# First modulation vectors of a two-block network: half as rows on VectorE, half as columns on TensorE, with the opening transfers on one queue

## The chip, the cores and the metric

The kernel runs on one core of one Trainium2 chip. The metric is the device time of one execution in microseconds (us), lower is better. The engines are PE (TensorE, matmuls), DVE (VectorE), ACT (ScalarE), POOL (GpSimd) and SP (SyncE, here only for issuing transfers). Each has its own instruction stream; they wait for one another on semaphores.

## What is computed

Two blocks of two layers each work on a sequence of 256 tokens of width 1024, all in float32; the first layer also carries a context sequence of 256 tokens. The prologue, which the change concerns, is the start of layer 0:

```python
m_lat = split(silu(c)     @ ada_w[0] + ada_b[0], 9)   # nine vectors of 1024: shift, scale, gate, ...
m_ctx = split(silu(c_ctx) @ ada_w[0] + ada_b[0], 9)
def half_ffn(h, m, off, g, w_gu, w_down):
    y = rmsnorm(h, g) * (1 + m[off + 1]) + m[off]
    return h + 0.5 * m[off + 2] * swiglu(y, w_gu, w_down)
h_ctx = half_ffn(ctx, m_ctx, 0, ...)                  # 256 tokens of the context
h_lat = half_ffn(x,   m_lat, 0, ...)                  # 256 tokens
```

Further on the context uses m_ctx[3] and m_ctx[4] for the mixer of layer 0. m_ctx[5] to m_ctx[8] reach no output, since nothing reads the context's residual after that mixer. Behind this stand the rest of four layers (mixers with scans, a convolution, gated linear attention, attention, and seven more feed-forward halves).

## The kernel before

Channels lie on the 128 partitions, so a vector of 1024 is 8 columns, called tiles here; the nine modulation vectors are MT = 72 tiles, in MOD[:, m, tile], with m = 0 for layer 0 and m = 4 for the context. X holds both sequences (the second is the context), Y the normalised input of the next product, PREW the first weights of the modulation (in ARENA), W two slots for weights, ADAW two slots for modulation rows, CB the vectors c and c_ctx copied to all partitions, CT the table of constants, VEC all small vectors.

The modulation is computed in two ways. The first 16 tiles (shift and scale of the first norm) are products on PE: `columns(c)` (L2377 to L2381), called for c = 0 to 3, has 4 blocks of 128 outputs by 8 blocks of the sum, each a 128x128 weight with a moving operand of only 2 columns (c and c_ctx); `first_mods` (L2722) adds the bias from PSUM. All other tiles are dot products by rows on DVE: `ada(g)` (L2689) takes a group of 4 tiles from an ADAW slot, multiplies each 128x1024 tile by the broadcast vector and accumulates, once for c_ctx into JUNK (L2705, layer 0 only) and once for c (L2708). POOL issues the loads of these groups, two ahead (L2333), and begins when PE has finished all four `columns`. The groups are spread over the feed-forward halves by lists of numbers, one for each unit; the first feed-forward takes 50 of the 68.

A feed-forward of both sequences has 11 units of gate and up products (L2402, four PSUM tiles of 128x512 each) and 4 units of down products (L2422).

The order before the first feed-forward is this. SP issues X, then four pieces of column weights, then the first weights. ACT issues VEC, CT and the two rows of CB, computes silu of c and c_ctx (L2650, L2651), squares X into Y (L2608), later takes the root (L2617) and silu of CB (L2675). PE waits for CT, runs `columns(0)` and `columns(1)`, then the sum of squares as 8 products with a matrix of ones (`total`, L2523), then `columns(2)` and `columns(3)`. DVE in `first_rms` inverts the root (L2919), normalises Y (L2922), waits in `first_mods`, forms the scales (L2937) and applies scale and shift to 16 blocks of 256 tokens (L2930). PE begins the first unit as soon as the first quarter of these is there.

Of the kernel before, what the change touches and what calls it, by code (L numbers as in the profile page):

```python
# [23 lines left out]
PRE_COLS = 512  # L24
PRE_TILES = PRE * PRE_COLS // P
GROUP = 4
SLOT = FT * 2 * P
# [21 lines left out]

ADA_GROUPS = [(0, tile) for tile in range(PRE_TILES, MT, GROUP)]  # L50
ADA_GROUPS += [(layer, tile) for layer in range(1, 4) for tile in range(0, MT, GROUP)]
LAYER_GROUPS = [sum(of <= layer for of, _ in ADA_GROUPS) for layer in range(4)]


def constant_table():
# [12 lines left out]
    add("ones", np.ones((P, P)))  # L68
    half = np.kron(np.eye(2), np.ones((HD, HD)))
# [42 lines left out]
    add("eps", np.tile(np.array([[1e-6, 64e-5, 1e-5 / ALPHA ** 2, 1e-5, 1.0, 0.0, np.pi / 2]]), (P, 1)))  # L112
# [41 lines left out]
def build(nc, t, out, table_at, stop=None):  # L154

    stop = STOP if stop is None else stop
    with ExitStack() as ctx:
# [6 lines left out]
        ncols = table_at["resident"][1]  # L164
# [44 lines left out]
        s_tab = sem("table_loaded")  # L209
# [519 lines left out]
        def rwkv_pe(pe, mm, ph):  # L729
            m = mixers["rwkv"]  # L730
            for seq in range(2):
# [6 lines left out]
                def tile(f):  # L738
# [8 lines left out]
                    if seq == 1 and n_ == 0:  # L747
                        pe.wait_ge(s_yl, 1)
# [1385 lines left out]
        group0 = 0  # L2134
# [46 lines left out]
        def norm(layer, k, T, of=None):  # L2181
            n_rs = sum_squares(T, 1.0 / D, "rms")
            if of:
                add("first_sums", of)
            n["nx"] += PIECES if n["y"] else 0
            add("rms", layer, 3 * k, T, n_rs, vec("norm_g", 24 * layer + 8 * k, 8), bump("y"), n["nx"])
# [142 lines left out]
        def _(pool):  # L2329
# [19 lines left out]
            for g in range(F[1]["group0"]):  # L2349
# [16 lines left out]
        def _(pe):  # L2366
# [18 lines left out]
            def ffn(sec, n_y):  # L2385
                T, w0, t0, per = sec["T"], sec["w0"], sec["t0"], sec["per"]

                def unit(u, dyn):
# [3 lines left out]
                    for q in range(2):  # L2392
                        for g in range(2):
# [132 lines left out]
            pe.wait_ge(s_tab, 16)  # L2526
            pe.wait_ge(s_sc, 1)
            columns(0)
            columns(1)
            first = True  # L2530
            for ph in phases:
                if ph[0] == "ffn":
                    ffn(F[ph[1]], ph[2])
                elif ph[0] == "small":
                    small_ffn(F[ph[1]], ph[2])
                elif ph[0] == "sum":
                    total(*ph[1:])
                    if first:
                        columns(2)
                        columns(3)  # L2540
# [16 lines left out]
        def _(act):  # L2557
# [95 lines left out]
            first = True  # L2653
            for ph in phases:
                if ph[0] == "ffn":
                    act.wait_ge(s_c2, 16)
# [7 lines left out]
                elif ph[0] == "rms":  # L2664
                    if ph[6] > PIECES:
                        rms(*ph[1:])
# [4 lines left out]
                elif ph[0] == "root":  # L2671
                    root(*ph[1:])
                    if first:
                        act.wait_ge(s_cb, 32)
                        A(CB[:, :], CB[:, :], ACT.Silu).then_inc(s_sc, 1)  # L2675
                        first = False
# [8 lines left out]
        def _(dve):  # L2685
# [3 lines left out]
            def ada(g, part=range(GROUP)):  # L2689
# [3 lines left out]
                if part[0] == 0 and g < g1:  # L2693
                    dve.wait_ge(s_adaw[g % 2], 16 * (g // 2 + 1))
                elif g >= g1:

                    whole = (g1 + 1 - g % 2) // 2
# [15 lines left out]
                if g + 1 in LAYER_GROUPS:  # L2713
                    dve.wait_ge(s_acc, g + 1)
                    a = PRE_TILES if layer == 0 else 0
                    for m in (0, 4) if layer == 0 else (layer,):
                        link(V.tensor_tensor(MOD[:, m, a:MT], MOD[:, m, a:MT], bias(layer)[:, a:MT], ALU.add))
# [198 lines left out]
            def first_rms(layer, k, T, n_rs, g, n_y, n_nx):  # L2916
# [8 lines left out]
                scales(layer, k, T, g)  # L2925
# [121 lines left out]
```

## Time and profile before

| | |
|---|---|
| median of 3 runs | 3244.76 us (3241.37 to 3246.73) |
| profiled execution, its own time | 3246.99 us |
| profiled execution, its span | 3245.2 us |
| busy: PE, DVE, ACT, POOL | 92%, 58%, 18%, 7% of the span |
| first feed-forward product on PE | 81.61 us after the span's start |
| mean rate of the transfers | 159 GB/s over the span |

In the profile each product of float32 operands shows as two records on PE, so `columns` c = 0 to 3 appear as 256 records and the sum as 16. A wait in brackets names what ended the idle time before an instruction. The span begins with the first instruction of any engine.

### The profile page before, as it was taken

How to read it: one execution, taken by the hardware profiler on the slowest of the kernel's cores; microseconds unless marked ns; L12 is line 12 of the kernel's file. 1: busy time of each engine (PE TensorE's matmuls, PEld its weight loads, DVE VectorE, ACT ScalarE, POOL GpSimd, SP SyncE). 2: the span in 40 equal slices, each digit the busy share in tenths (PEclk: the TensorE clock that was granted, in tenths of full speed). 3: DMA queues.
4: the chain of work that ended last, by engine and by line, in shares of the span. 5: the costliest groups of instructions: out<-in, count | busy, mean ns of one | idle time of the engine just before them, and what ended most of it. 6: DMA issues, size and time to landing. Idle time of an engine off the chain costs nothing.

```text
span 3245.2 us, 61069 instructions
## 1 busy us (share of the span) xinstructions
PE 2994.5 (92%) x26800; PEld 2565.2 (79%) x26800; DVE 1896.4 (58%) x3378; ACT 568.8 (18%) x1289; POOL 222.2 (7%) x363
## 2 busy tenths in 40 slices
PE   7999999777978899999999999999999989989898
PEld 6444444676677789999889999987779989976898
DVE  1777666543545368677556767744336657633674
ACT  1000001343333210100221011023211010031201
POOL 0000000331234000000000000000000000000000
PEclk8999999899889999999999999999999999998999
DMA  5668985101300346566425655634244535522453
GB/s 216 239 233 313 376 339 218 53 4 42 96 23 4 127 160 233 183 215 220 133 77 200 213 190 194 210 111 125 91 149 156 186 114 162 191 68 66 130 189 98
DMA packets 368962, 514.86 MB, mean 159 GB/s; under 512 B 11632, under 2 KB 350640, under 8 KB 361152
## 3 DMA queue, kind: packets, MB, share of 16 engines
q1 hardware_dynamic: 350992, 364.11, 34.6%
q0 software_dynamic: 17136, 144.19, 11.5%
q8 instruction: 207, 3.39, 0.4%
q10 hardware_dynamic: 576, 2.75, 0.2%
q14 instruction: 51, 0.42, 0.0%
HBM read 509.97 MB, written 1.05 MB: 157 GB/s over the span
## 4 chain that ended last, share of the span: by engine, by line
PE 83%; DVE 5%; DMA 4%; ACT 4%; issue 2%; POOL 1%; SPq 0%; DVEq 0%; ACTq 0%; POOLq 0%
PE PS L2472 28%; PE PS L2512 14%; PE PS L2402 7%; PE PS L580 5%; PE PS L600 5%; PE PS L2422 5%; PE PS L752 4%; PE PS L1643 2%; PE PS L1568 2%; PE PS L2523 2%; PE PS L2381 2%; DMA ADAW<-in_ada_rows 2%; DMA W<-in_ffn_w_down 1%; DVE ADAW L2708 1%; PE PS L1327 1%
## 5 line engine op out<-in xcount | busy, mean ns | idle before, releaser
L2472 PE MATMUL PS<-Y,W 128*128 128x128 f32 x4928 | 593.0, 279 | 43.6 <-ACT Y L2625 32.3
L2472 PEld LDWEIGHTS PS<-Y,W 128*128 128x128 f32 x4928 | 576.3, 195 | 49.4 <-issue 34.3
L2472 PE MATMUL PS<-Y,ARENA 128*128 128x128 f32 x3696 | 438.9, 275 | 0.0
L2472 PEld LDWEIGHTS PS<-Y,ARENA 128*128 128x128 f32 x3696 | 426.2, 192 | 0.0
L2402 PE MATMUL PS<-Y,W 128*128 128x512 f32 x704 | 304.0, 595 | 2.2 <-DVE Y L2930 2.2
L2512 PE MATMUL PS<-ARENA,W 128*128 128x128 f32 x2464 | 286.6, 275 | 8.2 <-DVE ARENA L2814 5.0
L2512 PEld LDWEIGHTS PS<-ARENA,W 128*128 128x128 f32 x2464 | 280.1, 192 | 10.1 <-DVE ARENA L2814 6.7
L2402 PEld LDWEIGHTS PS<-Y,W 128*128 128x128 f32 x704 | 134.3, 191 | 171.2 <-issue 170.7
L2708 DVE SCALAR_TENSOR_TENSOR ADAW<-ADAW,CB 128x1024 f32<-128x1024 f32 x200 | 238.7, 1221 | 27.7 <-DMA ADAW<-in_ada_rows 27.4
L600 PE MATMUL PS<-W 64*64 64x64 f32 x4608 | 118.6, 227 | 45.2 <-ACT W L849 24.5
L2422 PE MATMUL PS<-ARENA,W 128*128 128x512 f32 x352 | 154.3, 601 | 3.9 <-DVE ARENA L2762 3.9
L600 PEld LDWEIGHTS PS<-W 64*64 64x64 f32 x4608 | 105.3, 139 | 56.2 <-issue 27.2
L2785 DVE TENSOR_TENSOR ARENA<-W 128x1024 f32<-128x1024 f32 (+1 forms) x105 | 139.4, 1328 | 13.6 <-DMA W<-in_ffn_w_down 6.0
L2512 PE MATMUL PS<-ARENA 128*128 128x128 f32 x1232 | 146.7, 275 | 0.0
L580 PE MATMUL PS<-Y,W 128*128 128x256 f32 (+2 forms) x560 | 128.5, 393 | 19.1 <-ACT Y L2625 8.7
L752 PE MATMUL PS<-Y,W 128*128 128x256 f32 x560 | 132.7, 398 | 13.5 <-DMA W<-in_e_w_in 7.8
L2512 PEld LDWEIGHTS PS<-ARENA 128*128 128x128 f32 x1232 | 142.1, 192 | 0.0
L2422 PEld LDWEIGHTS PS<-ARENA,W 128*128 128x128 f32 x352 | 67.9, 193 | 90.3 <-issue 85.6
L580 PEld LDWEIGHTS PS<-Y,W 128*128 128x128 f32 (+2 forms) x560 | 108.1, 194 | 39.5 <-issue 10.1
L2790 DVE TENSOR_TENSOR ARENA<-ARENA,W 128x1024 f32<-128x1024 f32 (+1 forms) x105 | 139.1, 1325 | 0.2
L2794 DVE TENSOR_TENSOR W<-W 128x1024 f32<-128x1024 f32 (+1 forms) x105 | 139.1, 1325 | 0.0
L752 PEld LDWEIGHTS PS<-Y,W 128*128 128x128 f32 x560 | 110.4, 199 | 36.0 <-issue 20.0
(399 smaller groups left out, 3724.5 us busy)
## 6 DMA issues: line engine op xcount, KB each, us to landing
ADAW<-in_ada_rows POOLq DMA_DIRECT2D x52, 2048.0 KB, 9.0
W<-in_ffn_w_gu SPq DMA_DIRECT2D x88, 1024.0 KB, 8.2
W<-in_ffn_in SPq DMA_DIRECT2D x88, 1024.0 KB, 7.6
W<-in_ffn_w_down SPq DMA_DIRECT2D x32, 1408.0 KB, 11.3
W<-in_ffn_out SPq DMA_DIRECT2D x32, 1408.0 KB, 9.3
ADAW<-in_ada_rows POOLq DMA_DIRECT2D x64, 512.0 KB, 6.6
W<-in_even_w_in SPq DMA_DIRECT2D x40, 512.0 KB, 4.7
W<-in_e_w_in SPq DMA_DIRECT2D x34, 512.0 KB, 4.7
```

The costliest lines, as they stand in the source:

```text
L580: last = mm(PS[idx % 4][0:m_, 0:S], wide(c, kt, n_)[:, k, q * P:q * P + m_], x(k), start=(k == 0), stop=(k == kt - 1))
L600: last = mm(to, x, y, start=(k == 0), stop=(k == len(pairs) - 1))
L752: last_ = mm(PS[at[f] % 4][:, 0:S], wide(c, DT, cols)[:, k, q * P:(q + 1) * P], Y[:, k, off:off + S], start=(k == 0), stop=(k == DT - 1))
L1568: last = mm(PS[idx % 4][:, 0:S], wide(c, DT)[:, k, (i % 2) * P:(i % 2 + 1) * P], Y[:, k, 0:S], start=(k == 0), stop=(k == DT - 1))
L2402: last = mm(o, gate_up(c)[:, g, k, q * P:(q + 1) * P], Y[:, k, 0:T], start=(k == 0), stop=(k == DT - 1))
L2422: last = mm(PS[idx % 4][:, 0:T], wide(c, FT)[:, k, q * P:(q + 1) * P], H[:, k, 0:T], start=(k == 0), stop=(k == FT - 1))
L2472: last = mm(block_bank(b, q), w[left][:, k, q * P:(q + 1) * P], YB[right][:, k], start=(k == 0 and p not in (2, 5)), stop=(k == 3), skip_g ...
L2512: last = mm(block_bank(b, 0), w[left][:, k], HB[right][:, k], start=(k == 0 and p not in (2, 5)), stop=(k == PAIRS - 1), skip_group_check= ...
L2708: ins = V.scalar_tensor_tensor(w, w, 1.0, c_rows, ALU.mult, ALU.mult, accum_out=MOD[:, layer, tile + i:tile + i + 1])
L2785: V.tensor_tensor(w["S1"], w["A21"], w["A22"], ALU.add).then_inc(s_s1, 1)
L2790: V.tensor_tensor(w["S2"], w["S1"], w["A11"], ALU.subtract).then_inc(s_s2, 1)
L2794: V.tensor_tensor(w["S3"], w["A11"], w["A21"], ALU.subtract).then_inc(s_s3, 1)
```

## The change

The 16 first tiles are split. The shift vector (tiles 0 to 7) stays on PE: PRE_COLS falls from 512 to 256, so each of the four pieces is 1 MB instead of 2 MB. The scale vector (tiles 8 to 15) becomes two groups of rows (HEAD = 2), which DVE computes in a new `head()` before anything else; they use the two ADAW slots, and their loads are issued by SP. Silu of CB moves on ACT ahead of the squares. The table is cut in two, and only its first 263 columns are loaded ahead. SP issues nearly all the opening transfers, ACT only the first part of the table. PE runs one `columns` ahead of the sum and three behind it. In the first norm, scale and shift of the context are done by ACT, of the first sequence by DVE, and PE waits for both by quarters. Context products are left out for tiles from 40 on, which nothing reads. Two groups more stand in the list, both in `head()`; the first feed-forward takes 50 groups as before.

```diff
-PRE_COLS = 512
+PRE_COLS = 256
+HEAD = 2
+CTX_TILES = 5 * D // P
+HEAD_TILES = PRE_TILES + HEAD * GROUP
...
-        group0 = 0
+        group0 = HEAD
...
         @block.sync
         def _(sp):
-            sp.dma_start(X[:, :, :, :].rearrange("p s k n -> p (s k n)"), t["xT"]).then_inc(s_x, 16)
-            for c in range(PRE):
+            def columns(c):
                 sp.dma_start(PREW[:, c].rearrange("p k n -> p (k n)"), t["ada_columns"][c * P:(c + 1) * P, :])\
                     .then_inc(s_pre[c], 16)
+
+            def first_rows(g):
+                sp.dma_start(ADAW[:, g].rearrange("p a b -> p (a b)"), t["ada_rows"][g * P:(g + 1) * P, :])\
+                    .then_inc(s_head[g], 16)
+
+            sp.dma_start(VEC[:, :], t["vectors"]).then_inc(s_vec, 16)
+            for i, name in enumerate(("c", "c_ctx")):
+                sp.dma_start(CB[:, i], t[name].to_broadcast([P, D])).then_inc(s_cb, 16)
+            first_rows(0)
+            columns(0)
+            sp.dma_start(X[:, :, :, :].rearrange("p s k n -> p (s k n)"), t["xT"]).then_inc(s_x, 16)
+            first_rows(1)
+            for c in range(1, PRE):
+                columns(c)
+            sp.dma_start(CT[:, early:ncols], t["table"][:, early:ncols]).then_inc(s_rest, 16)
...
-            for g in range(F[1]["group0"]):
+            for g in range(HEAD, F[1]["group0"]):
                 rows(g)
...
                                 if u == 0 and q == 0 and g == 0 and k % (DT // PIECES) == 0:
                                     pe.wait_ge(s_y, n_y - PIECES + 1 + k // (DT // PIECES))
+                                    pe.wait_ge(s_yl, 1 + k // (DT // PIECES))
...
-            pe.wait_ge(s_tab, 16)
             pe.wait_ge(s_sc, 1)
             columns(0)
-            columns(1)
+            pe.wait_ge(s_tab, 16)
...
                 if ph[0] == "ffn":
+                    pe.wait_ge(s_rest, 16)
                     ffn(F[ph[1]], ph[2])
...
                     if first:
-                        columns(2)
-                        columns(3)
+                        for c in range(1, PRE):
+                            columns(c)
...
-            act.dma_start(VEC[:, :], t["vectors"]).then_inc(s_vec, 16)
-            act.dma_start(CT[:], t["table"][:, 0:ncols]).then_inc(s_tab, 16)
-            for i, name in enumerate(("c", "c_ctx")):
-                act.dma_start(CB[:, i], t[name].to_broadcast([P, D])).then_inc(s_cb, 16)
+            act.dma_start(CT[:, 0:early], t["table"][:, 0:early]).then_inc(s_tab, 16)
             act.wait_ge(s_vec, 16)
             A(SC[:, 0, :], vec("c", 0, DT), ACT.Silu)
             A(SC[:, 1, :], vec("c_ctx", 0, DT), ACT.Silu).then_inc(s_sc, 1)
+            act.wait_ge(s_cb, 32)
+            A(CB[:, :], CB[:, :], ACT.Silu).then_inc(s_sc, 1)
...
                 elif ph[0] == "rms":
-                    if ph[6] > PIECES:
-                        rms(*ph[1:])
+                    rms(*ph[1:])
...
-                    if layer == 0:
+                    if layer == 0 and tile < CTX_TILES:
...
+            def head():
+
+                dve.wait_ge(s_sc, 2)
+                for g in range(HEAD):
+                    ada(g)
+                dve.wait_ge(s_acc, HEAD)
+                for m in (0, 4):
+                    of = MOD[:, m, PRE_TILES:HEAD_TILES]
+                    link(V.tensor_tensor(of, of, bias(0)[:, PRE_TILES:HEAD_TILES], ALU.add))
...
                 first_mods()
                 scales(layer, k, T, g)
+
+                V.tensor_scalar(GS[:, 1, :], GS[:, 1, :], 1.0, None, ALU.mult).then_inc(s_nx, PIECES)
                 for i in range(0, DT, kt):
-                    for s, m in ((0, layer), (1, 4)):
-                        for j in range(i, i + kt):
-                            y = Y[:, j, s * S:(s + 1) * S]
-                            ins = V.tensor_scalar(y, y, GS[:, s, j:j + 1], MOD[:, m, 8 * k + j:8 * k + j + 1],
-                                                  ALU.mult, ALU.add)
-                    ins.then_inc(s_y, 1)
+                    for j in range(i, i + kt):
+                        y = Y[:, j, 0:S]
+                        ins = V.tensor_scalar(y, y, GS[:, 0, j:j + 1], MOD[:, layer, 8 * k + j:8 * k + j + 1],
+                                              ALU.mult, ALU.add)
+                    ins.then_inc(s_yl, 1)
                 dve.wait_ge(s_y, n_y)
...
             dve.wait_ge(s_vec, 16)
+            head()
```

How the instructions stand now at three places. First the transfers that SP issues at the program's start, up to the first weights W; before:

```order
L2257 DMA X<-in_xT 128x4096
L2259 DMA ARENA<-in_ada_columns 128x4096 x4
L2270 DMA W<-in_ffn_w_gu 128x8x256 x4
```

and with the change:

```order
L2272 DMA VEC<-in_vectors 128x811
L2274 DMA CB<-in_c 128x1024
L2274 DMA CB<-in_c_ctx 128x1024
L2269 DMA ADAW<-in_ada_rows 128x4096
L2265 DMA ARENA<-in_ada_columns 128x2048
L2277 DMA X<-in_xT 128x4096
L2269 DMA ADAW<-in_ada_rows 128x4096
L2265 DMA ARENA<-in_ada_columns 128x2048 x3
L2281 DMA CT<-in_table 128x2249
L2291 DMA W<-in_ffn_w_gu 128x8x256 x4
```

X, one group of rows and a quarter of the columns stand ahead of the rest, and three small transfers have come over from ACT's queue.

Second, PE from its start to the first feed-forward unit (names in brackets are the semaphores waited for); before:

```order
L2381 MATMUL PS<-SC,ARENA 128x2 [waits first_modulation_weights_loaded0,silu_c_ready,table_loaded]
L2381 MATMUL PS<-SC,ARENA 128x2 x31
L2381 MATMUL PS<-SC,ARENA 128x2 [waits first_modulation_weights_loaded1]
L2381 MATMUL PS<-SC,ARENA 128x2 x31
L2523 MATMUL PS<-Y,CT 128x512 [waits squares_ready]
...
L2381 MATMUL PS<-SC,ARENA 128x2 [waits first_modulation_weights_loaded2]
L2381 MATMUL PS<-SC,ARENA 128x2 x31
L2381 MATMUL PS<-SC,ARENA 128x2 [waits first_modulation_weights_loaded3]
L2381 MATMUL PS<-SC,ARENA 128x2 x31
```

and with the change:

```order
L2402 MATMUL PS<-SC,ARENA 128x2 [waits first_modulation_weights_loaded0,silu_c_ready]
L2402 MATMUL PS<-SC,ARENA 128x2 x15
L2545 MATMUL PS<-Y,CT 128x512 [waits squares_ready,first_of_table_loaded]
...
L2402 MATMUL PS<-SC,ARENA 128x2 [waits first_modulation_weights_loaded1]
L2402 MATMUL PS<-SC,ARENA 128x2 x15
L2402 MATMUL PS<-SC,ARENA 128x2 [waits first_modulation_weights_loaded2]
L2402 MATMUL PS<-SC,ARENA 128x2 x15
L2402 MATMUL PS<-SC,ARENA 128x2 [waits first_modulation_weights_loaded3]
L2402 MATMUL PS<-SC,ARENA 128x2 x15
L2429 UNCONDITIONAL_BRANCH [waits rest_of_table_loaded]
```

Ahead of the sum 16 small products are left of 64, behind it 48 of 64.

Third, DVE from its start; before:

```order
L2919 RECIPROCAL RS<-RS 128x512 [waits root_ready,vectors_loaded]
L2922 TENSOR_TENSOR Y<-X,RS 128x2x256 [waits vector_chain] x8
L2728 TENSOR_TENSOR MOD<-PS,VEC 128x4 [waits dense_tile_done,vector_chain]
...
L2937 SCALAR_TENSOR_TENSOR GS<-MOD,VEC 128x8 [waits vector_chain]
L2930 TENSOR_SCALAR Y<-Y,GS,MOD 128x256 [waits vector_chain]
L2930 TENSOR_SCALAR Y<-Y,GS,MOD 128x256 x15
```

and with the change:

```order
L2723 SCALAR_TENSOR_TENSOR JUNK,MOD<-ADAW,CB 128x1024 [waits first_modulation_rows_loaded0,silu_c_ready,vectors_loaded]
L2726 SCALAR_TENSOR_TENSOR ADAW,MOD<-ADAW,CB 128x1024
...
L2723 SCALAR_TENSOR_TENSOR JUNK,MOD<-ADAW,CB 128x1024 [waits products_thrown_away,first_modulation_rows_loaded1]
L2726 SCALAR_TENSOR_TENSOR ADAW,MOD<-ADAW,CB 128x1024
...
L2745 TENSOR_TENSOR MOD<-MOD,VEC 128x8 [waits modulation_group_done]
L2745 TENSOR_TENSOR MOD<-MOD,VEC 128x8 [waits vector_chain]
L2947 RECIPROCAL RS<-RS 128x512 [waits root_ready,vector_chain]
L2950 TENSOR_TENSOR Y<-X,RS 128x2x256 [waits vector_chain] x8
...
L2955 TENSOR_SCALAR GS<-GS 128x8 [waits vector_chain]
L2959 TENSOR_SCALAR Y<-Y,GS,MOD 128x256 x8
```

Sixteen products of 128x1024 and two additions stand ahead of the reciprocal, and 8 of the 16 blocks of the last step have gone to ACT.

## Rows read from the trace of the kernel before

**Rows 1.** Chain of waits, pieces in order of time: start us, us, what

```profile
1.20 16.23 DMA CT<-in_table
17.48 27.47 PE PS L2381 x128
44.94 9.92 PE PS L2523 x16
54.87 24.53 PE PS L2381 x128
81.61 221.61 PE PS L2402 x512
304.03 9.17 DVE ADAW L2708 x16
313.49 10.10 DMA ADAW<-in_ada_rows
389.54 154.27 PE PS L2422 x352
```

**Rows 2.** Timeline: start us, us, engine line op [idle before, releaser]

```profile
17.45 4.26 ACT L2608 ACTIVATE Y<-X 128x512 f32<-128x512 f32 x8 [7.62 <-DMA CT<-in_table]
54.90 0.69 ACT L2617 ACTIVATE RS<-PS,CT 128x512 f32<-128x512 f32 x1 [31.89 <-PE PS L2523]
55.70 3.35 DVE L2919 RECIPROCAL RS<-RS 128x512 f32<-128x512 f32 x1 [55.70 <-ACT RS L2617]
56.90 1.91 ACT L2675 ACTIVATE CB<-CB 128x2048 f32<-128x2048 f32 x1
59.09 5.78 DVE L2922 TENSOR_TENSOR Y<-X,RS 128x512 f32<-128x512 f32 x8
79.42 0.16 DVE L2728 TENSOR_TENSOR MOD<-PS,VEC 128x4 f32<-128x4 f32 x1 [13.42 <-PE PS L2381]
80.09 5.26 DVE L2930 TENSOR_SCALAR Y<-Y,GS,MOD 128x256 f32<-128x256 f32 x16
```

**Rows 3.** PE by stretches: us, busy (records), granted clock, DMA share, GB/s

```profile
17.40:44.80 27.40, 27.32 (x128) 1.00 1.03 391
44.80:51.00 6.20, 6.20 (x9) 1.00 0.17 54
51.00:54.70 3.70, 3.70 (x10) 1.00 0.00 0
54.70:57.00 2.30, 2.30 (x23) 1.00 0.00 0
59.00:79.40 20.40, 20.38 (x96) 0.50 0.00 1
```

**Rows 4.** Opening transfers: size each, us from issue to landing

```profile
X<-in_xT SPq DMA_DIRECT2D x1, 2048.0 KB, 8.6
CT<-in_table ACTq DMA_DIRECT2D x1, 1256.0 KB, 16.2
ARENA<-in_ada_columns SPq DMA_DIRECT2D x1, 2048.0 KB, 27.6
CB<-in_c_ctx ACTq DMA_DIRECT2D x1, 512.0 KB, 27.8
ARENA<-in_ada_columns SPq DMA_DIRECT2D x1, 2048.0 KB, 31.9
W<-in_ffn_w_gu SPq DMA_DIRECT2D x1, 1024.0 KB, 37.9
```

**Rows 5.** Timeline: when SP and ACT issued those of rows 4

```profile
0.76 0.39 SPq L2257 DMA_DIRECT2D X<-in_xT  x1
1.20 0.45 ACTq L2646 DMA_DIRECT2D CT<-in_table  x1
2.14 0.69 SPq L2259 DMA_DIRECT2D ARENA<-in_ada_columns  x1
2.16 0.77 ACTq L2648 DMA_DIRECT2D CB<-in_c_ctx  x1
2.87 0.60 SPq L2259 DMA_DIRECT2D ARENA<-in_ada_columns  x1
4.02 24.62 SPq L2270 DMA_DIRECT2D W<-in_ffn_w_gu  x1
```

**Rows 6.** Timeline of DVE: ends of the first group of rows

```profile
89.61 1.22 DVE L2705 SCALAR_TENSOR_TENSOR JUNK<-ADAW,CB 128x1024 f32<-128x1024 f32 x1 [4.27 <-DMA ADAW<-in_ada_rows]
98.79 0.68 DVE L2762 TENSOR_TENSOR ARENA<-SIL,PS 128x512 f32<-128x512 f32 x1
```

**Rows 7.** Timeline: scale and shift on ACT in the second norm

```profile
554.02 4.04 ACT L2625 ACTIVATE Y<-Y,MOD,GS 128x256 f32<-128x256 f32 x8 [2.62 <-DVE Y L2943]
```

**Rows 8.** Waits of PE, 80 to 620 us: total us, times, longest

```profile
PE PS L2422 <- DVE ARENA L2762: 3.9, 1, 3.9
```

**Rows 9.** Transfers issued alone or in pairs: size, us to landing

```profile
ARENA<-in_c POOLq DMA_DIRECT2D x1, 512.0 KB, 4.8
ADAW<-in_ada_rows POOLq DMA_DIRECT2D x52, 2048.0 KB, 9.0
W<-in_ffn_w_gu SPq DMA_DIRECT2D x88, 1024.0 KB, 8.2
```

More of the change, by code:

```diff
@@ L68, in constant_table @@
     add("ones", np.ones((P, P)))
+    add("eps", np.tile(np.array([[1e-6, 64e-5, 1e-5 / ALPHA ** 2, 1e-5, 1.0, 0.0, np.pi / 2]]), (P, 1)))
+    at["early"] = (0, n)
     half = np.kron(np.eye(2), np.ones((HD, HD)))
@@ L111, in constant_table @@
     add("spread", head.T)
-    add("eps", np.tile(np.array([[1e-6, 64e-5, 1e-5 / ALPHA ** 2, 1e-5, 1.0, 0.0, np.pi / 2]]), (P, 1)))
     at["resident"] = (0, n)
@@ L162, in sem @@
             return ctx.enter_context(nc.semaphore(name))
-        ncols = table_at["resident"][1]
+        ncols, early = table_at["resident"][1], table_at["early"][1]
         CT = sb("CT", [P, ncols])
@@ L208, in build @@
         s_vec = sem("vectors_loaded")
-        s_tab = sem("table_loaded")
+        s_tab = sem("first_of_table_loaded")
+        s_rest = sem("rest_of_table_loaded")
+        s_head = [sem(f"first_modulation_rows_loaded{i}") for i in range(HEAD)]
         s_x = sem("x_loaded")
@@ L747, in tile @@
                     if seq == 1 and n_ == 0:
-                        pe.wait_ge(s_yl, 1)
+                        pe.wait_ge(s_yl, PIECES + 1)
                     for k in range(DT):
@@ L2184, in norm @@
                 add("first_sums", of)
-            n["nx"] += PIECES if n["y"] else 0
+            n["nx"] += PIECES
             add("rms", layer, 3 * k, T, n_rs, vec("norm_g", 24 * layer + 8 * k, 8), bump("y"), n["nx"])
@@ L2651, in _ @@
             A(SC[:, 1, :], vec("c_ctx", 0, DT), ACT.Silu).then_inc(s_sc, 1)
+            act.wait_ge(s_cb, 32)
+            A(CB[:, :], CB[:, :], ACT.Silu).then_inc(s_sc, 1)
             act.wait_ge(s_tab, 16)
-            first = True
             for ph in phases:
                 if ph[0] == "ffn":
+                    act.wait_ge(s_rest, 16)
                     act.wait_ge(s_c2, 16)
@@ L2672, in _ @@
                     root(*ph[1:])
[L2673 to L2676, printed above, removed]
                 elif ph[0] == "do":
@@ L2692, in ada @@
                 g1 = F[1]["group0"] + 2
-                if part[0] == 0 and g < g1:
-                    dve.wait_ge(s_adaw[g % 2], 16 * (g // 2 + 1))
+                if g < HEAD:
+                    dve.wait_ge(s_head[g], 16)
+                elif part[0] == 0 and g < g1:
+                    dve.wait_ge(s_adaw[g % 2], 16 * ((g - HEAD) // 2 + 1))
                 elif g >= g1:
-                    whole = (g1 + 1 - g % 2) // 2
+                    whole = (g1 - HEAD + 1 - g % 2) // 2
                     dve.wait_ge(s_adaw[g % 2], 16 * (whole + GROUP * ((g - g1) // 2) + GROUP))
@@ L2714, in ada @@
                     dve.wait_ge(s_acc, g + 1)
-                    a = PRE_TILES if layer == 0 else 0
-                    for m in (0, 4) if layer == 0 else (layer,):
-                        link(V.tensor_tensor(MOD[:, m, a:MT], MOD[:, m, a:MT], bias(layer)[:, a:MT], ALU.add))
+                    a = HEAD_TILES if layer == 0 else 0
+                    for m, b in ((0, MT), (4, CTX_TILES)) if layer == 0 else ((layer, MT),):
+                        link(V.tensor_tensor(MOD[:, m, a:b], MOD[:, m, a:b], bias(layer)[:, a:b], ALU.add))
+            def head():
[6 more added lines that the diff above has]
+                    link(V.tensor_tensor(of, of, bias(0)[:, PRE_TILES:HEAD_TILES], ALU.add))
             def bias(layer):
```

## The prediction

> **What bounds the kernel now.** I began with the page's shares: PE is busy 92% of the span, so what counts is when PE starts dense work and whether it then ever waits. The chain of waits in order of time answers the first [rows 1]: a table transfer to 17.4, PE's small products to 44.9, the sum of squares to 54.9, small products again to 79.4, and the first feed-forward product at 81.61. Everything ahead of that product is prologue. The waits of PE from 80 to 620 us answer the second [rows 8]: in the whole first feed-forward PE stands still once, 3.9 us at 389 us, behind a chain in which DVE's row products and the loads of rows follow each other [rows 1]. That chain has no link with the clock time of the prologue, so it moves with the start. The question is thus how much earlier than 81.61 the first dense product comes.
>
> The stretches of PE give the price of the small products [rows 3]. Ahead of the sum 128 records take 27.4 us, 0.214 us each. Behind it the first 23 take 2.3 us, 0.100 each, and then 96 take 20.4 us, 0.213 each. So just after the sum PE runs at its upper level for some 2.3 us and then at the lower. The sum itself has about 8 records of twice the length of the last 8. The column of the granted clock reads 1.00 in the slow first stretch too, so I go by the length of records: 0.85 against 0.43 us for a sum record is 1.2 against 2.4 GHz.
>
> Last I read the landings of the opening transfers [rows 4] with their issue times [rows 5]. X (2.10 MB, with VEC 0.42 MB beside it) is in at 0.76+8.6 = 9.4, the table (by then 5.9 MB in all) at 17.4, the third piece of columns and the second row of CB (11.1 MB) at 29.7 and 30.0, the last piece, alone on its queue (13.2 MB), at 34.8. All of these lie on one line: **landing = 3.5 us + bytes / 0.42 MB per us** (9.5, 17.5, 30.0, 35.0). One queue alone held this rate over the last 2.1 MB, 4.9 us.
>
> **The transfers after the change, by that line.** Sizes are in the order of the instructions. VEC and the first table part 0.55 MB: 4.8 us. Both rows of CB, 1.60 in all: 7.3. First rows 3.70: 12.3. First columns 4.74: 14.8. X 6.84: 19.8. Second rows 8.94: 24.8. The other three columns 9.99, 11.04, 12.08: 27.3, 29.8, 32.3. Rest of the table 13.24: 35.0. The first weights W come after the same 13.24 MB as before, so they land as before, at 4.02+37.9 = 41.9. SP's issues cost 0.4 to 0.7 us each, 11 of them ahead of W, some 6 us, and the transfers drain more slowly than that.
>
> **PE.** Its first 16 products are 32 records of 0.214: 14.8 to 21.7. The squares on ACT start at 19.8 and take 4.26 for 8 [rows 2], so the first quarter is there at 20.9, the last at 24.1, and the sum at the lower level needs 1.7 us a quarter: no wait. It costs what it cost, 9.9 [rows 1]: ends 31.7. Then 96 records: 23 at 0.100 and 73 at 0.213, 17.9 us: PE ends its small products at **49.6**. The columns have landed by 32.3, so it never waits for them. Removed against before are 128 records: the 96 that no longer precede the sum, and 32 of those behind it.
>
> **DVE.** The rows need silu of CB: 7.3 plus 1.9 [rows 2], 9.2. One group is 8 products in 98.79 - 89.61 = 9.2 us [rows 6]. First group 12.3 to 21.5; second from its landing, 24.8 to 34.0; two small additions, 34.6. The root is ready at 31.7 + 0.7 = 32.4, so DVE is the later one there by 2.2 us. Reciprocal and the 8 normalising products take from 55.70 to 64.87 before, 9.2 [rows 2]: 43.8. Then it waits for PE until 49.6, so the head on DVE has 5.8 us of cover and costs nothing. If that cover went, each us beyond it would be paid in full.
>
> **From PE's last small product to the first dense one.** Before, 79.42 to 81.61, 2.2 us: additions, scales, then four blocks of 0.33 for the first quarter. Now there is one chained small operation more, about 0.2, then ACT's two blocks of the context, 4.04/8 = 0.5 each [rows 7], against DVE's two of 0.33. Together 2.4 us: first dense product at **52.0**, 10 us behind the first weights and 17 behind the rest of the table, so those new waits cost nothing. PE takes 3.4 us for a quarter at the lower level and ACT 1.0, so later quarters are there in time. The start of the feed-forward at the lower level is the same in both.
>
> **Behind it.** DVE now waits for ACT's last block, 4.0 us after its start, before it begins row products; their loads are issued by POOL when PE ends its small products, as before, and arrive some 9 us later [rows 9], so that wait is hidden by them. The left-out context products are 32 of 1.15 us, 37 us of DVE, in the first eight units; PE never waited for DVE there, so they are worth 0. They end before the chain at 304 us begins, so the 3.9 us stay. Bounds: nothing, or 3.9 if the chain gets shorter. The additions and waits at the second norm are the same in number.
>
> **Sum.** 81.6 - 52.0 = 29.6 us. Against the profiled execution, 3246.99 (span 3245.2, 1.8 us around it), that is 3217.4; that execution lies 2.2 above the median, so against the median of 3244.8 I say **3215.2**. One measurement of this kernel can tell 0.2%, 6.5 us, from no change.
>
> **A rule against a row.** PE was busy 27.3 of 27.4 us with small products and stayed at the lower level [rows 3]. The Trainium skill, TensorE: Matmul & The Clock Gate, section Part 1, says that the throttled state is the default and that activity releases it; with activity read as a busy engine, the small products would run at 2.4 GHz, and all PE work here would halve. By that rule the trace disagrees, and I keep 0.214 in the sum; the case is a rival below.
>
> **The rivals.**
> - *PE at its upper level throughout, DVE becomes the bound.* From rows: the small products ahead 3.2 us; the sum 6.8 from 20.9, ended 27.7; 96 records of 0.100 end at 37.3. DVE, at 43.8, is then last, 0.4 for the additions and 2.0 from scales to product: 46.2, so 3209.4. For it: records at 0.100 stand right behind the sum. Against it: they last only 2.3 us, and 128 records before the sum never got there. Chance 0.07.
> - *PE at its lower level throughout.* The sum takes 16 times 0.85, 13.6, ended 35.3; 96 records 20.4, ended 55.7; product at 58.1: 3221.3. For it: where the rise falls is not mine to compute, and less dense work precedes it now only in small products. Chance 0.09.
> - *The front of the queue is slow.* The two rows of CB read one row of memory 128 times. They never ran alone; the nearest row is the same transfer for c_2, 4.8 us to landing with nothing before it [rows 9], against 2.5 for both here. At 4.8 each everything behind is 7.1 later: columns 21.9, sum from 28.7 to 38.6, end 56.5, product 58.9: 3222.1. Chance 0.13.
> - *Slower than before: one queue serves its transfers one after another, each only when the last has landed.* Then lone landing times add up: three of 0.4 to 0.5 MB at 4.8, three of 2 MB at 9.0, seven of 1 MB at 8.2 (four columns, the table, two W) [rows 9], 98.8 us; W is last, first product near 99.5 instead of 81.6: 3262.7. It decides once W lands after 88, 6.8 us a transfer. Against it: the last two columns landed 5.1 us apart (29.7 and 34.8), not 9. Chance 0.02.
> - *The gain is given back in the first feed-forward*, its end set by loads: 3244.8. 3.9 us of waits in 460 speak against it. Chance 0.03.
>
> **How the numbers follow.** The forecast has the rest, 0.66, with its own range 3211 to 3220: the 2.2 us between execution and median, some 2 us for where the level changes, and the 3.9 us stall. The range for 8 in 10 reaches down to the fast clock and up to the slow front with some 3 us of the spread of the runs: 3208 to 3225. Faster by over 0.2%: all but the last two, 0.95; within 0.2%: 0.03; slower: 0.02.
>
> **What would show it.** In the profile after: X in near 20 us; sum on PE from about 22 to 32; last small product near 49.6, and DVE's addition behind it waiting on PE for about 6 us; first dense product near 52 with ACT's block as its releaser; the first feed-forward 462 us long with one stall near 360 us. I am wrong if DVE is the one waited for (rows products late or longer than 9.2 a group), if X lands past 25, or if the first feed-forward grows by what was won.

## The result, and the profile after

The changed kernel takes **3209.98 us** (median of 4 runs, 3207.45 to 3213.30) against 3243.07 before on the same chip (4 runs): the ratio is 0.9892, 95% interval 0.9878 to 0.9906, some 33 us less, where the forecast had 29.6 less. The forecast was 3215.2 with a range of 3208 to 3225; the time lies in it, 1 us below the forecast case's own 3211 to 3220. The profiled execution took 3208.70 us, its span is 3206.9.

The chain of waits of the changed kernel, pieces in order of time (start us, us, what), answers to [rows 1]:

```profile
2.61 13.44 DMA ARENA<-in_ada_columns
16.19 6.96 PE PS L2402 x32
23.15 9.20 PE PS L2545 x16
32.35 15.26 PE PS L2402 x96
49.78 304.88 PE PS L2424 x704
355.81 151.33 PE PS L2444 x352
507.13 6.88 PE PS L2545 x16
```

The opening is still on PE from the first piece of columns on, and the first dense product comes at 49.78 instead of 81.61, 31.8 us earlier. The down products (L2444) take 151.33 instead of 154.27. The second norm's sum begins at 507.13, against 543.82 in the first profile before. From the first dense product to there it is 457.4 us, where the prediction had 462.

The timeline of the same stretch (columns as in [rows 2]):

```profile
13.71 1.22 DVE L2723 SCALAR_TENSOR_TENSOR JUNK<-ADAW,CB 128x1024 f32<-128x1024 f32 x1 [13.71 <-DMA ADAW<-in_ada_rows]
21.05 4.27 ACT L2630 ACTIVATE Y<-X 128x512 f32<-128x512 f32 x8 [10.55 <-DMA X<-in_xT]
25.87 1.22 DVE L2723 SCALAR_TENSOR_TENSOR JUNK<-ADAW,CB 128x1024 f32<-128x1024 f32 x1 [2.90 <-DMA ADAW<-in_ada_rows]
35.56 3.35 DVE L2947 RECIPROCAL RS<-RS 128x512 f32<-128x512 f32 x1
44.76 0.16 DVE L2756 TENSOR_TENSOR MOD<-PS,VEC 128x2 f32<-128x2 f32 x1
47.64 0.16 DVE L2756 TENSOR_TENSOR MOD<-PS,VEC 128x2 f32<-128x2 f32 x1 [2.39 <-PE PS L2402]
48.59 4.04 ACT L2647 ACTIVATE Y<-Y,MOD,GS 128x256 f32<-128x256 f32 x8 [15.51 <-DVE GS L2955]
```

DVE's rows run from 13.7 to 35.0 with one gap of 2.9 us for the second group; the normalising is over at 44.7, and DVE then still waits 2.4 us for PE's last small product. So PE is the bound, as forecast, and the cover of DVE is thinner than the 5.8 us of the prediction.

What is left of the one stall [rows 8], from the waits of PE between 40 and 590 us:

```profile
PE PS L2424 <- ACT Y L2647: 2.2, 1, 2.2
PE PS L2444 <- DVE ARENA L2790: 1.2, 1, 1.2
```

Steps of the sum, in us of the profiled execution:

| step | forecast | measured |
|---|---|---|
| first rows, first columns, X, second rows in | 12.3, 14.8, 19.8, 24.8 | 13.7, 16.2, 21.0, 25.9 |
| PE's first 32 records | 14.8 to 21.7 | 16.2 to 23.2 |
| sum, then 96 records | 9.9 + 17.9 | 9.2 + 15.3 |
| PE's last small product | 49.6 | 47.6 |
| DVE's normalising done | 43.8 | 44.7 |
| from there to the first dense product | 2.4 | 2.2 |
| first dense product | 52.0 | 49.8 |
| stall ahead of the down products | 3.9 | 1.2 |

Two things were open: why PE's part was shorter by 3.3 us, and whether the shorter stall (with the quicker down products behind it, 2.7 + 2.9 us) belongs to the change.

### The profile page after: what moved, and what is told of

Same layout as the page of the kernel before. It is cut to its first block, busy times and chain, and to the rows that moved or that the text cites. A ratio compares the mean times of both kernels' runs of the same rounds, so it can differ in the third digit from the quotient of the medians.

```text
span 3206.9 us, 60800 instructions
## 1 busy us (share of the span) xinstructions
PE 2965.7 (92%) x26672; PEld 2537.7 (79%) x26672; DVE 1876.3 (59%) x3341; ACT 573.0 (18%) x1297; POOL 222.4 (7%) x363
## 3 DMA queue, kind: packets, MB, share of 16 engines
HBM read 509.97 MB, written 1.05 MB: 159 GB/s over the span
## 4 chain that ended last, share of the span: by engine, by line
PE 86%; DVE 4%; ACT 4%; DMA 3%; issue 2%; POOL 1%; SPq 0%; DVEq 0%; ACTq 0%; POOLq 0%
PE PS L2494 28%; PE PS L2534 15%; PE PS L2424 10%; PE PS L587 5%; PE PS L607 5%; PE PS L2444 5%; PE PS L759 4%; PE PS L1650 2%; PE PS L1575 2%; PE PS L2545 1%; DMA W<-in_ffn_w_down 1%; PE PS L1334 1%; PE PS L623 1%; PE PS L1428 1%; PE PS L2402 1%
## 5 line engine op out<-in xcount | busy, mean ns | idle before, releaser
L2424 PE MATMUL PS<-Y,W 128*128 128x512 f32 x704 | 304.9, 596 | 2.2 <-ACT Y L2647 2.2
L2534 PEld LDWEIGHTS PS<-ARENA,W 128*128 128x128 f32 x2464 | 280.1, 192 | 8.8 <-DVE ARENA L2842 6.2
L2726 DVE SCALAR_TENSOR_TENSOR ADAW<-ADAW,CB 128x1024 f32<-128x1024 f32 x208 | 246.5, 1221 | 14.7 <-DMA ADAW<-in_ada_rows 14.4
L607 PE MATMUL PS<-W 64*64 64x64 f32 x4608 | 118.8, 227 | 43.5 <-ACT W L856 24.5
L2444 PE MATMUL PS<-ARENA,W 128*128 128x512 f32 x352 | 151.3, 592 | 1.2 <-DVE ARENA L2790 1.2
L587 PEld LDWEIGHTS PS<-Y,W 128*128 128x128 f32 (+2 forms) x560 | 108.0, 194 | 38.7 <-issue 10.1
L2619 ACT ACTIVATE SIL<-SIL 128x256 f32<-128x256 f32 x77 | 32.1, 417 | 583.0 <-DVE SIL L2885 583.0
```

The lines of the kernel that those rows point to most:

```text
L587: last = mm(PS[idx % 4][0:m_, 0:S], wide(c, kt, n_)[:, k, q * P:q * P + m_], x(k), start=(k == 0), stop=(k == kt - 1))
L607: last = mm(to, x, y, start=(k == 0), stop=(k == len(pairs) - 1))
L2444: last = mm(PS[idx % 4][:, 0:T], wide(c, FT)[:, k, q * P:(q + 1) * P], H[:, k, 0:T], start=(k == 0), stop=(k == FT - 1))
L2534: last = mm(block_bank(b, 0), w[left][:, k], HB[right][:, k], start=(k == 0 and p not in (2, 5)), stop=(k == PAIRS - 1), skip_group_check= ...
L2726: ins = V.scalar_tensor_tensor(w, w, 1.0, c_rows, ALU.mult, ALU.mult, accum_out=MOD[:, layer, tile + i:tile + i + 1])
```

## The experiments

Ten kernels were run. In the table, "first dense" is the start of the first feed-forward product, "sum + small" the sum and the small products behind it until the last, as the chain has them (for e4 the timeline), added dense products among them, both from the one profiled execution; the median is over all runs.

| kernel | median us | first dense | sum + small | stall | down products |
|---|---|---|---|---|---|
| before | 3243 to 3244 | 81.6 | 9.9 + 24.5 | 3.9 | 154.3 |
| before again (e8) | 3240.2, one run | 78.7 | 8.8 + 22.5 | 2.0 | 151.3 |
| before, context left out (e2) | 3243.7 | 78.4 | 8.9 + 22.4 | 5.4 | 153.8 |
| changed | 3210.0 | 49.8 | 9.2 + 15.3 | 1.2 | 151.3 |
| changed again (e8b) | 3212.4 | 50.0 | 8.5 + 15.9 | 1.2 | 151.3 |
| context kept (e1) | 3211.8 | 49.6 | 8.6 + 15.9 | 1.2 | 151.3 |
| norm on DVE (e3) | 3212.3 | 52.8 | 9.9 + 17.7 | 1.2 | 151.3 |
| old order, two queues (e4) | 3221.8 | 60.9 | 10.0 + 17.8 | 1.8 | 151.3 |
| all 16 tiles on PE (e5) | 3241.1 | 77.4 | 9.3 + 38.7 | 2.7 | 151.3 |
| dense product each 8 (e6) | 3221.6 | 54.8 | 9.0 + 20.7 | 2.2 | 153.0 |
| dense product each 16 (e7) | 3219.8 | 54.7 | 8.4 + 21.1 | 1.2 | 151.3 |
| columns first (e9) | 3215.7 | 52.1 | 9.7 + 18.0 | 1.2 | 151.3 |

### Are the left-out context products worth anything? (e1, e2)

```diff
 e1, on the changed kernel
-CTX_TILES = 5 * D // P
+CTX_TILES = MT
 e2, on the kernel before
-                    if layer == 0:
+                    if layer == 0 and tile < 40:
...
-                    for m in (0, 4) if layer == 0 else (layer,):
-                        link(V.tensor_tensor(MOD[:, m, a:MT], MOD[:, m, a:MT], bias(layer)[:, a:MT], ALU.add))
+                    for m, b in ((0, MT), (4, 40)) if layer == 0 else ((layer, MT),):
+                        link(V.tensor_tensor(MOD[:, m, a:b], MOD[:, m, a:b], bias(layer)[:, a:b], ALU.add))
```

> The change with the context products of tiles 40 to 71 kept. In the changed kernel PE's one stall in the first feed-forward was 1.2 us instead of 3.9, and the down products behind it took 2.9 us less. Theory A (the left-out products are worth nothing; the shorter stall is scatter in the landing of rows): first dense product at 49.8, time as the changed kernel's within 3 us, the stall anywhere from 0 to 4 us. Rival B (the left-out products shorten the chain on DVE): stall back at 3.9, down products slower again, 5 to 6 us longer than the changed kernel.

> The kernel before with only those context products left out. Theory A: first dense product at 81.6, the time of before within 3 us, DVE less busy by 37 us. Rival B: the stall falls from 3.9 to about 1 us and the time by 5 to 6 us.

Measured: e1 3211.83 us, ratio to before 0.9903 (0.9886 to 0.9920), as the changed kernel; e2 3243.73 us, ratio 0.9998 (0.9989 to 1.0006). The first dense product of e2, expected at 81.6, came at 78.4, although the edit changes nothing ahead of it: its sum and small products took 31.3 us instead of 34.5. That difference comes back in e8, where nothing was edited. The waits of PE, first of e1, then of e2:

```profile
PE PS L2444 <- DVE ARENA L2790: 1.2, 1, 1.2
```

```profile
PE PS L2422 <- DMA W<-in_ffn_w_down: 5.4, 1, 5.4
```

With all products kept the stall stays at 1.2, and with them left out of the old kernel it is 5.4, released there by a load of down weights. DVE's busy time in the first feed-forward does fall: e1 has 56 products for the context there and e2 has 24 (68.3 and 29.2 us), and neither median moves beyond its interval. B falls; the 37 us of DVE work are worth nothing that these runs could tell, as the prediction had it.

### Is the short stall a property of the new prologue? (e8, e8b)

Both kernels once more, without an edit.

> The kernel before once more, one look. PE's stall ahead of the down products in the first feed-forward was 3.9 us in the first profile and 5.4 with the context products left out (there behind a load of down weights), and 1.2 to 2.7 in the six kernels with the new prologue. Theory A (scatter of the landings from execution to execution): any value from 1 to 5.5 us here. Rival C (the old prologue causes the long stall): 3.5 us or more again. The sum and the small products behind it took 34.4 and 31.3 us in two executions of this prologue, so the first dense product comes between 78 and 82.

> The changed kernel once more. Sum plus small products took 24.4 and 24.5 us in two executions of this prologue and 27.6 in a third (16 sum records and 96 small ones in all three), depending on where PE's level rises and falls: first dense product between 49.5 and 52.8. Stall: 1 to 2.7 under C, 1 to 5.5 under A. Time 3207 to 3214.

Measured: e8 3240.23 us in its one execution; e8b 3212.43 us, ratio 0.9897 (0.9880 to 0.9913). Chain and waits of e8:

```profile
17.78 27.47 PE PS L2381 x128
45.25 8.79 PE PS L2523 x16
54.04 22.45 PE PS L2381 x128
78.71 222.07 PE PS L2402 x512
385.20 151.33 PE PS L2422 x352
536.53 6.88 PE PS L2523 x16
```

```profile
PE PS L2422 <- DVE ARENA L2762: 2.0, 1, 2.0
```

The old prologue, too, can have a stall of 2.0 and down products of 151.3. "3.5 us or more again", rival C, is out. What remains is, as far as is known, scatter in the landings of rows and weights; but three executions of the old prologue had 2.0, 3.9 and 5.4 and nine of the new 1.2 to 2.7, so a smaller part on the new one's side is not excluded, and I have no mechanism for it. The down products are slower by 1.7 to 2.9 us in three of the four executions whose stall was over 2.1 us, and in no other. In the 5 us from the first down product on, the granted clock was 0.50 in the first profile before and in e2, and 0.66 in e6; in the fourth, e5 with a stall of 2.7, it was 1.00 and nothing was paid.

For the change, e8 against e8b is the better pair, since both have the short sum and small products: the first dense product moves by 78.71 - 50.04 = 28.7 us, and the second norm's sum from 536.53 to the 506.72 of e8b:

```profile
50.04 221.81 PE PS L2424 x512
355.39 151.33 PE PS L2444 x352
506.72 6.88 PE PS L2545 x16
```

29.8 us, where the first pair showed 36.7. Two executions with the long value give the same shift of the start, 81.61 - 52.76 (e3, below) = 28.9. The 31.8 us of the first pair set a long one against a short one. e8b's whole span is 3216.0 all the same, 9.1 longer than that of the first profile, although it is level with it at the second norm; it falls behind in the mixer that follows, by 3.2 us at 590 us, 7.1 at 755 and 9.0 at 863. The windows of PE from 600 to 650 us (busy, granted clock, DMA share, GB/s), first of the changed kernel, then of e8b:

```profile
600.00:650.00 50.00, 40.18 (x1429) 0.89 0.01 4
```

```profile
600.00:650.00 50.00, 38.35 (x1256) 0.80 0.02 3
```

The mixer's small products ran with a mean granted clock of 0.80 instead of 0.89 there. So executions differ by several us in places that the change doesn't touch, with PE's level at least a part of it, and two single profiles can't be subtracted to better than that. From the second norm to the end the three executions of the old kernels take 2701 to 2707 us and the nine of the new ones 2698 to 2709: behind that norm no gain shows.

### What the transfers' order is worth, and what the rows on DVE (e4, e5)

```diff
 e4, on the changed kernel: SP
-            sp.dma_start(VEC[:, :], t["vectors"]).then_inc(s_vec, 16)
-            for i, name in enumerate(("c", "c_ctx")):
-                sp.dma_start(CB[:, i], t[name].to_broadcast([P, D])).then_inc(s_cb, 16)
-            first_rows(0)
-            columns(0)
             sp.dma_start(X[:, :, :, :].rearrange("p s k n -> p (s k n)"), t["xT"]).then_inc(s_x, 16)
-            first_rows(1)
-            for c in range(1, PRE):
+            for c in range(PRE):
                 columns(c)
-            sp.dma_start(CT[:, early:ncols], t["table"][:, early:ncols]).then_inc(s_rest, 16)
+            for g in range(HEAD):
+                first_rows(g)
 e4, ACT
+            act.dma_start(VEC[:, :], t["vectors"]).then_inc(s_vec, 16)
             act.dma_start(CT[:, 0:early], t["table"][:, 0:early]).then_inc(s_tab, 16)
+            act.dma_start(CT[:, early:ncols], t["table"][:, early:ncols]).then_inc(s_rest, 16)
+            for i, name in enumerate(("c", "c_ctx")):
+                act.dma_start(CB[:, i], t[name].to_broadcast([P, D])).then_inc(s_cb, 16)
 e5, on the changed kernel; head(), first_rows() and their calls go too
-PRE_COLS = 256
-HEAD = 2
+PRE_COLS = 512
+HEAD = 0
```

> The change with the transfers in the old order on two queues: on SP X, the four columns, then both groups of rows; on ACT VEC, table, CB. Theory (landing by bytes in order at 0.42 MB per us): second rows land near 35, DVE ends its rows near 48.5, has 9.2 us more to do, and is the last: first dense product near 60.7, 10 to 11 us later than with the change. Rival (the order of transfers matters little, PE's small products set the start): 49.8.

> The change with all 16 first tiles on PE again (four pieces of 2 MB, no rows on DVE ahead), new order and queue kept. Theory (small products on PE are the price): 64 products ahead are 32 now, in records 64 ahead of the sum and 192 behind; first piece in near 13.5, sum from 27 to 36.5, the rest at 0.213 a record after some 27 fast ones, ended near 74.7, first dense product near 77: 27 us later than with the change, so that the new order alone is worth 4 to 5 us. Rival (the order of transfers is the gain): near 55 to 60.

Measured: e4 3221.80 us, ratio 0.9936 (0.9917 to 0.9954); e5 3241.12 us, ratio 0.9991 (0.9981 to 1.0001). The timeline of e4:

```profile
25.47 1.91 ACT L2671 ACTIVATE CB<-CB 128x2048 f32<-128x2048 f32 x1 [15.55 <-DMA CB<-in_c_ctx]
28.56 10.12 PE L2540 MATMUL PS<-Y,CT 128*128 128x512 f32 x16 [9.24 <-ACT Y L2625]
30.35 1.22 DVE L2722 SCALAR_TENSOR_TENSOR JUNK<-ADAW,CB 128x1024 f32<-128x1024 f32 x1 [30.35 <-DMA ADAW<-in_ada_rows]
49.20 3.35 DVE L2946 RECIPROCAL RS<-RS 128x512 f32<-128x512 f32 x1
60.94 29.47 PE L2419 MATMUL PS<-Y,W 128*128 128x512 f32 x63 [4.63 <-ACT Y L2642]
```

The first rows are in at 30.3, as the line of landings has them (30.0), the reciprocal starts at 49.2, and the first dense product comes at 60.9, forecast 60.7: now DVE is the last. It also shows a cost that I hadn't counted: ACT meets the silu of CB ahead of the squares, so the late rows of CB hold up the squares and with them the sum, to 28.6, though X had landed with the first transfers. It was hidden, since DVE was later still. The chain of e5:

```profile
13.37 13.78 PE PS L2395 x64
27.15 9.34 PE PS L2538 x16
36.49 38.72 PE PS L2395 x192
77.38 222.77 PE PS L2417 x512
```

First dense product at 77.4, forecast 77. The new order and queue alone are thus worth 4.2 us against the first profile of before and 1.3 against e8. The 4.2 compares like with like: e5's sum and small products are 48.1 us, the 34.5 of the first profile plus 64 records of 0.213. The ratio says 0 to 6 us and can't tell either from no change. Rows on DVE with the old order bring 20.7 or 17.8. Both together bring 28.7 to 28.9 between executions of like length. So beside the rows on DVE the new order and queue are worth 8 to 11 us (60.9 against 52.8 or 49.8; the medians say 9 to 12), since the rows then stand in time, and without them some 4. No run separates the order from the number of queues.

### Is the norm on two engines worth anything? (e3)

```diff
                 elif ph[0] == "rms":
-                    rms(*ph[1:])
+                    if ph[6] > PIECES:
+                        rms(*ph[1:])
...
-                V.tensor_scalar(GS[:, 1, :], GS[:, 1, :], 1.0, None, ALU.mult).then_inc(s_nx, PIECES)
                 for i in range(0, DT, kt):
-                    for j in range(i, i + kt):
-                        y = Y[:, j, 0:S]
-                        ins = V.tensor_scalar(y, y, GS[:, 0, j:j + 1], MOD[:, layer, 8 * k + j:8 * k + j + 1],
-                                              ALU.mult, ALU.add)
-                    ins.then_inc(s_yl, 1)
+                    for s, m in ((0, layer), (1, 4)):
+                        for j in range(i, i + kt):
+                            y = Y[:, j, s * S:(s + 1) * S]
+                            ins = V.tensor_scalar(y, y, GS[:, s, j:j + 1], MOD[:, m, 8 * k + j:8 * k + j + 1],
+                                                  ALU.mult, ALU.add)
+                    ins.then_inc(s_y, 1)
```

The waits on PE that belong to it go back too.

> The change with all 16 blocks of scale and shift on DVE again. Theory: the first quarter is 4 blocks of 0.33 on DVE against 2 of 0.5 on ACT and one chained operation, so the first dense product stays at 49.8 within 0.3 us and the time is the same. Rival: two engines save half of the 5.3 us that the 16 blocks take, so one engine costs 2.6 us.

Measured: 3212.34 us, ratio 0.9906 (0.9888 to 0.9923). The first dense product came at 52.8, 3 us later than with the change, which looks like the rival. The chain and the wait say otherwise:

```profile
22.92 9.90 PE PS L2544 x16
32.82 17.72 PE PS L2402 x96
52.76 303.99 PE PS L2423 x704
```

```profile
PE PS L2423 <- DVE Y L2959: 2.2, 1, 2.2
```

The wait ahead of the product is the same 2.2 us. The 3 us arose before it, in the sum and the small products (27.6 against 24.5), which the edit doesn't touch; e8 and e2 against the first profile show the same 3 us without any such edit. Two engines instead of one are worth nothing here, since PE needs only the first quarter.

### PE's level in the small products (e6, e7)

```diff
                         last = mm(PS[c][:, 2 * q:2 * q + 2], PREW[:, c, k, q * P:(q + 1) * P], SC[:, :, k],
                                   start=(k == 0), stop=(k == DT - 1))
+                    if c and (c * (PRE_COLS // P) + q) % 1 == 0:
+                        mm(PS[7][:, :], PREW[:, c, 0, q * P:(q + 1) * P], X[:, 0, 0:2].rearrange("p a b -> p (a b)"),
+                           start=True, stop=True)
```

The condition holds for each of the six blocks behind the sum; e7 has `% 2` in its place, which holds for three.

> The change with a dense product thrown away (512 columns of X, into an unused bank) after every 8 small products behind the sum, 6 in all. Theory L (small products run at the lower level because little passes through the array, dense work keeps the upper): all records at 0.100 and 0.43, 14.7 us instead of 15.3, small products end near 47 and the feed-forward begins without its slow first records (2.5 us less). Rival M (the level does not depend on what the products are, only on time since the start or on PE being busy): records stay at 0.213, the 12 dense records come on top with 5 to 10 us.

> The same with a dense product after every 16 small ones, 3 in all. Theory L: 96 times 0.100 and 6 times 0.43, 12.2 us, ended near 44.5, DVE (45.2) becomes the bound, first dense product near 47.4, and perhaps no slow first records: 2 to 5 us less than the change. If three dense products are too few to hold the level: records at 0.213 in part, 3 to 5 us more than the change. Rival M: 3 to 5 us more in any case.

Measured: e6 3221.63 us, ratio 0.9926 (0.9909 to 0.9943); e7 3219.78 us, ratio 0.9925 (0.9908 to 0.9942). The chain of e6, L2405 the added products:

```profile
23.00 9.01 PE PS L2548 x16
32.02 1.68 PE PS L2402 x16
33.70 0.97 PE PS L2405 x2
...
37.31 1.68 PE PS L2402 x16
38.98 0.97 PE PS L2405 x2
39.95 2.47 PE PS L2402 x16
42.42 1.92 PE PS L2405 x2
44.34 3.20 PE PS L2402 x16
```

Two pieces of e7, between its added products:

```profile
34.06 4.77 PE PS L2402 x32
40.75 6.62 PE PS L2402 x32
```

In e6 three groups of 16 records take 1.68 us each, 0.105 a record, then the level falls, the later groups take 3.20, and an added product 1.92 instead of 0.97. By the granted clock, which goes there from 1.00 (2.4 GHz) to 0.50 (1.2 GHz), the level fell at 40.6 us in e6 and at 36.0 in e7. With small products alone it fell at 37.7 in the changed kernel and between 34.4 and 36.7 in e1, e3, e8b and e9.

L fails: with six dense products the level fell all the same, and with three of them not even later. M's price came true, 5 us at the first dense product in both (54.8 and 54.7 against 49.8), and its records at 0.213 only in part, since they stayed fast until 40.6 in e6. Whether the dense products held the level there is not shown: it is one execution, and without them the place moves by over 3 us. The medians lie 7 to 12 us above the changed kernel's two, more than these 5; e7's profiled execution was the fastest of its four, and where the rest arises is not shown.

### A better order? (e9)

```diff
-            first_rows(0)
             columns(0)
+            first_rows(0)
...
                         for c in range(1, PRE):
                             columns(c)
+                        mm(PS[7][:, :], PREW[:, 3, 0, 0:P], X[:, 0, 0:2].rearrange("p a b -> p (a b)"),
+                           start=True, stop=True)
```

> The change with the first piece of columns ahead of the first rows on the queue, and one dense product thrown away behind the last small product, in the 2.2 us in which PE waits for the first quarter of Y. Theory: PE's first small products run at 11 to 18 instead of 16 to 23; X lands unchanged near 21, so the sum starts with the first squares at 22.1 instead of 23.0, 0.9 us earlier, and so does everything on PE; rows land at 16.2 instead of 13.7, end at 25.4 and not earlier than the second rows land (25.9), so DVE is unchanged at 45.2 and just covered. The dense product lets PE's level rise 2 us earlier, up to 0.9 us. In all 0.9 to 1.8 us less than the change, below what the times can tell (6 us), to be read in the trace. Rival: the wait ahead of the first dense product is not free for the extra product, 1 us more.

Measured: 3215.70 us, ratio 0.9917 (0.9899 to 0.9935). Its timeline:

```profile
11.23 6.96 PE L2402 MATMUL PS<-SC,ARENA 128*128 128x2 f32 x32 [11.23 <-DMA ARENA<-in_ada_columns]
22.25 9.72 PE L2545 MATMUL PS<-Y,CT 128*128 128x512 f32 x16 [4.06 <-ACT Y L2632]
31.80 18.16 PE L2402 MATMUL PS<-SC,ARENA 128*128 128x2 f32 x96
52.14 10.15 PE L2424 MATMUL PS<-Y,W 128*128 128x512 f32 x20 [0.26 <-ACT Y L2649]
```

The sum starts at 22.25 instead of 23.0, 0.8 us earlier (forecast 0.9), and the added product fits into the wait, which ends with 0.26 us. The second part, an earlier rise of the level, can't be told: the first 10.2 us of the dense work hold 21 records against 18 in the changed kernel, but 20 in e3 and e8b too. Sum and small products took 27.7, the long value, and the first dense product came at 52.1, against 52.8 in e3. So the 0.8 us are there and can't be seen in the time; this is no version that beats the changed kernel.

## Why the prediction was right, point by point

**The place of the gain** was right: PE's small products bound the opening, DVE's rows fit beside them, and the start of the dense work moved by 28.7 to 28.9 us between like executions (31.8 in the first pair), forecast 29.6. e5 shows that without the rows on DVE it is 77.4.

**The line of landings** was right in slope and late by 1.2 us in offset. The issue and landing rows of the changed kernel (size, us from issue; issued at 0.76, 1.67 and 3.26):

```profile
VEC<-in_vectors SPq DMA_DIRECT2D x1, 405.5 KB, 4.1
CB<-in_c_ctx SPq DMA_DIRECT2D x1, 512.0 KB, 6.9
X<-in_xT SPq DMA_DIRECT2D x1, 2048.0 KB, 17.7
```

VEC is in at 4.9, on the line. The two rows of CB are in at 8.6, where the line says 7.3: 1.05 MB took 3.7 us and not 2.5. That is the rival of the slow front in direction, with 1.2 us instead of 7.1; that the repeated reading of one row is the reason is not isolated by a run. Everything behind is late by 1.1 to 1.4 us. Two readings of the prediction are off without effect: 41.9 is the landing of the second piece of W (the first lands at 38.9 before and 39.1 after), and the last 2.1 MB took 4.8 to 5.1 us by the rows.

**PE's price** is where the profile left the sum: 27.8 us for the sum and 96 records, measured 24.5. This is chance more than a wrong size. I took it from the one execution of before at hand, where sum and small products took 34.5; two other executions of the same prologue took 31.3. With the new prologue it was 24.4 or 24.5 in three executions and 27.6 to 27.8 in three (e3, e4, e9). It is thus one of two lengths some 3 us apart, in either kernel, as PE's level rises within the sum and falls within the small products. The forecast is right for the long one: 52.0, plus 1.2 for the late landings, less 0.2 each for PE's work and the last step, is the 52.8 of e3. The profiled execution of the changed kernel had the short one, and that is the difference between 52.0 and 49.8, less the late landings. What the prediction lacked is that the term has two values; the level's change was in its range with some 2 us. The rival of the upper level throughout did not come: behind 38 us the granted clock was 0.50 and the records were at 0.213.

**DVE** had normalised at 44.7 instead of 43.8, for the late rows, and then had 0.4 us of additions for the first three pieces, which the prediction had left out; it waited 2.4 us, and 4.8 or 5.5 with the long value of PE (e9, e3). The two-engine norm at nothing: confirmed by the wait in e3. The left-out context products at nothing: no effect in e1 and e2.

**Behind the start** I kept the 3.9 us stall and allowed for its going. It went to 1.2 in the profile, but to 2.0 in e8 without any change. The measured gain is 33.1 us here, 31.6, 31.1 and 31.4 in e1, e3 and e8b; the shift of the start gives 28.7 to 28.9 of it. The rest, 2 to 4 us, may be chance: the intervals of e1, e3 and e8b begin at 25 to 28 us, that of the first comparison at 30. It may also be the stretch from the first dense product to the second norm, 457.8 to 463.7 us in three executions of the old kernels and 456.2 to 459.2 in nine of the new, with their stalls. Or the short value of PE came oftener with the new prologue. That this part belongs to the change is not shown, and by the shift alone the time would have been nearer to the forecast.

**The rivals on the other side** failed plainly: transfers on one queue stream behind one another (X, 2 MB and sixth in line, in at 21.0), and the first feed-forward didn't give back the gain: 304.9 us of gate products against 304.0 before (389.54 less the stall of 3.94, less 81.61, [rows 1]).

## What to carry to other kernels

In an opening that is bound by one engine, give part of its work to an idle one in the form that suits that one, and put the transfers in the order in which both need them; here the order and queue alone were worth some 4 us by the trace (the times can't tell it from nothing), the split with the old order 18 to 21, both together 29. Landings of queued transfers could be worked out here to within 1.4 us from bytes and one rate. Before subtracting two profiles, take one more of each: a single execution carried 3 us of PE's level in the sum, up to 3.4 us of a stall and 9 us in a mixer that nothing had touched.

## What the runs showed of the hardware

- Products with a moving operand of 2 columns ran at 0.213 us a record although PE was busy without a gap, and at 0.100 only behind dense work. The column of the granted clock showed the slow records at 0.50 behind the sum, but at 1.00 ahead of it, with the same 0.213 a record. With six dense products among them the upper level lasted until 40.6 us in one execution (e6) and then fell all the same; with three it fell at 36.0 (e7), with none at 34.4 to 37.7 in five executions.
- The same program had its sum and small products in 31.3 or 34.5 us (before) and in 24.4 or 27.7 us (changed): PE's level rises and falls at different places from one execution to the next.
- Two broadcasts of one row of 4 KB to 128 partitions (1.05 MB) took 3.7 us on the queue, where the next MB of column weights took 2.5 (landings at 13.7 and 16.2 us).
